# Wide experts of a mixture-of-experts layer: weights loaded two k-tiles by 1024 columns, column blocks worked in pairs, two buffers for activated gate and product

## What is computed

```python
def swiglu(h, w1, w3, w2):
    return (jax.nn.silu(h @ w1) * (h @ w3)) @ w2

def moe_swiglu(h, router_w, w1, w3, w2):
    logits = (h @ router_w).astype(jnp.float32)
    top_val, top_idx = lax.top_k(logits, TOP_K)
    gates = jax.nn.softmax(top_val, axis=-1)
    dense_gate = jnp.sum(jax.nn.one_hot(top_idx, N_EXPERTS, dtype=jnp.float32) * gates[..., None], axis=-2).astype(h.dtype)
    out = jnp.zeros_like(h)
    for e in range(N_EXPERTS):
        out = out + dense_gate[..., e:e + 1] * swiglu(h, w1[e], w3[e], w2[e])
    return out
```

## Time and profile before

| | |
|---|---|
| median of three runs | 1856.14 us |
| the profiled execution | 1855.47 us |
| its span, first to last instruction | 1853.6 us |
| mean granted TensorE clock | 0.977 |
| TensorE busy in the span | 1697.7 us (92%) |
| VectorE, ScalarE | 851.4 us (46%), 742.3 us (40%) |
| mixture-of-experts stage | about 912 to 1850 us |
| one wide and one narrow expert | 232.3 us (from 1041.1 to 1273.4 us) |

### The profile page before, as it was taken

How to read it: one execution, slowest core, us unless ns; L and a number is a source line. 1 busy time by engine, 2 the same in 40 slices (tenths; PEclk the granted TensorE clock), 3 DMA queues, 4 the chain that set the end, 5 groups by cost and what they waited for, 6 DMA issues and landing times.

```text
span 1853.6 us, 22005 instructions
## 1 busy us (share of the span) xinstructions
PE 1697.7 (92%) x9050; PEld 1201.8 (65%) x9050; DVE 851.4 (46%) x994; ACT 742.3 (40%) x918; POOL 26.1 (1%) x27
## 2 busy tenths in 40 slices
PE   6998898999999989989999977999779997799976
PEld 5877585888888868757778523885238852388622
DVE  4334726232233354263798402884028840288401
ACT  5332535222232235355677302773027730277301
POOL 0000000000000001030000000000000000000000
PEclk9999998999999999999899999999999999999999
DMA  9644133632223245162799899998999989999896
GB/s 336 202 161 135 46 114 121 210 102 91 92 99 105 91 153 171 37 180 92 269 336 376 335 409 394 377 386 333 409 395 390 369 339 409 394 374 382 336 410 267
DMA packets 238637, 473.82 MB, mean 256 GB/s; under 512 B 16121, under 2 KB 115377, under 8 KB 238529
## 3 DMA queue, kind: packets, MB, share of 16 engines
q1 hardware_dynamic: 238144, 471.38, 70.3%
q0 software_dynamic: 384, 0.95, 0.2%
HBM read 471.25 MB, written 1.05 MB: 255 GB/s over the span
## 4 chain that ended last, share of the span: by engine, by line
PE 73%; DMA 17%; DVE 5%; ACT 3%; issue 1%; SPq 1%; ACTq 0%; DVEq 0%
PE bank L608 19%; PE bank L609 19%; PE bank L610 19%; DMA raw_weights<-in_moe_w 16%; PE bank L2460 4%; PE bank L675 2%; PE bank L2477 1%; PE bank L2356 1%; PE bank L2395 1%; PE bank L465 1%; DMA raw_weights<-in_ev_w_in 1%; PE bank L888 1%; ACT split_high L587 1%; DVE split_low L1802 1%; PE bank L683 1%
## 5 line engine op out<-in xcount | busy, mean ns | idle before, releaser
L608 PE MATMUL bank<-h_high,split_high 128*128 128x512 f32 (+1 forms) x832 | 317.1, 381 | 7.4 <-DVE h_low L522 3.9
L609 PE MATMUL bank<-h_low,split_high 128*128 128x512 f32 (+1 forms) x832 | 314.4, 378 | 0.0
L610 PE MATMUL bank<-h_high,split_low 128*128 128x512 f32 (+1 forms) x832 | 314.1, 378 | 0.0
L1802 DVE TENSOR_TENSOR split_low<-raw_weights,split_high 128x2048 fp32r<-128x2048 f32 x112 | 256.3, 2289 | 79.2 <-ACT split_high L1548 78.4
L592 DVE TENSOR_TENSOR split_low<-raw_weights,split_high 128x1024 fp32r<-128x1024 f32 x118 | 144.0, 1225 | 292.3 <-ACT split_high L587 292.3
L1548 ACT ACTIVATE split_high<-raw_weights 128x2048 fp32r<-128x2048 f32 x110 | 211.0, 1918 | 77.7 <-PE bank L610 75.0
L2460 PE MATMUL bank<-raw_weights,xe_narrow 128*64 128x512 f32 (+1 forms) x1024 | 209.2, 546 | 36.0 <-DMA raw_weights<-in_moe_w 35.4
L587 ACT ACTIVATE split_high<-raw_weights 128x1024 fp32r<-128x1024 f32 x118 | 124.1, 1056 | 188.8 <-PE bank L610 183.5
L608 PEld LDWEIGHTS bank<-h_high,split_high 128*128 128x128 f32 x832 | 158.5, 191 | 40.8 <-issue 7.7
L2460 PEld LDWEIGHTS bank<-raw_weights,xe_narrow 128*64 128x64 f32 x1024 | 67.9, 136 | 168.7 <-issue 89.5
L610 PEld LDWEIGHTS bank<-h_high,split_low 128*128 128x128 f32 x832 | 158.4, 190 | 28.8
(11 more groups left out here) (303 smaller groups left out, 2225.4 us busy)
## 6 DMA issues: line engine op xcount, KB each, us to landing
raw_weights<-in_moe_w SPq DMA_DIRECT2D x336, 1024.0 KB, 8.5
raw_weights<-in_w_mod SPq DMA_DIRECT2D x48, 1024.0 KB, 6.3
raw_weights<-in_ffn_w SPq DMA_DIRECT2D x33, 1024.0 KB, 5.3
raw_weights<-in_ev_w_in SPq DMA_DIRECT2D x10, 1024.0 KB, 10.2
raw_weights<-in_od_w_in SPq DMA_DIRECT2D x8, 1024.0 KB, 6.7
raw_weights<-in_ev_w_out SPq DMA_DIRECT2D x4, 1024.0 KB, 7.1
raw_weights<-in_od_w_out SPq DMA_DIRECT2D x4, 1024.0 KB, 8.2
overlay<-in_rpb SPq DMA_DIRECT2D x32, 64.0 KB, 3.0
```

The costliest lines, as they stand in the source:

```text
L608: pe.matmul(ps, wh, xh, start=first, stop=False)
L609: pe.matmul(ps, wh, xl, start=False, stop=False)
L610: return pe.matmul(ps, wl, xh, start=False, stop=last)
L1802: dve.tensor_tensor(lo, RAW[:, u % NRAW, :], hi.bitcast(F32), ALU.subtract).then_inc(S("e_low"), 1)
```

## The change

All experts, wide and narrow, now share the order by pairs of blocks. For a wide expert:

- **Units.** A unit of `a` or `b` is two k-tiles by 1024 columns (4 KB pieces) and serves both blocks of a pair; pair 3 (block 6) keeps four k-tiles by 512 columns. The number of units, 42, the six raw buffers and the three pairs of split buffers stay.
- **Order.** a0 b0 a1 b1 d0 a2 b2 d1 a3 b3 d2 d3 by pairs, with four units in an item of pairs 0 to 2 and two in one of pair 3. A pair uses PSUM banks 0 and 2 (`a`) and 1 and 3 (`b`), the next pair the same ones again, with waits for `esilu` and `ge_free` per block.
- **Turns.** `turn(2p - 2)` stands behind the first half of the units of `a` of pair p, `turn(2p - 1)` behind the second half. For pairs 1 and 2 that is two units apart, for pair 3 one. `turn` itself has the same waits as before.
- **ScalarE and VectorE.** The silus, the high and low parts of the turned product and the products are put behind units by formulas in `u`.
- **Buffers.** `GE` and `SIL` become two each; the second ones lie in `MROW`, which is free by then. `silu` and `product` wait for one block less.
- **Seams.** The combination behind a narrow expert uses banks 1, 3, 6 and 7, as it now falls into the middle of the first `a` item. `gather` moves behind the low part of unit 4 (it was behind unit 3). `turn_onehots` comes behind unit 7 (it was behind unit 3), the `gates` behind unit 14 (it was behind unit 11).

Numbers of instructions on TensorE, ScalarE, VectorE and of DMAs don't change. The core of the diff, first the units and the buffers:

```diff
+def blocks(p):
+
+    return tuple(j for j in (2 * p, 2 * p + 1) if j < JE)
+
+def pair_units(p):
+
+    return 2 * len(blocks(p))
...
+        GE = [X[:, 4:6, 0:256], MROW[:, 0, :].rearrange("p (a n) -> p a n", a=2)]
+        SIL = [X[:, 6:8, 0:256], MROW[:, 1, :].rearrange("p (a n) -> p a n", a=2)]
...
+                    k, n, c = (2, 1024, 1024 * p) if pair_units(p) == 4 else (4, 512, 1024 * p)
```

ScalarE:

```diff
+                    for u in range(NU):
+                        if u >= 2 or b or e:
                             act.wait_ge(*raw_full(b, e, u))
                             act.wait_ge(S("e_slots"), NU * wide_before(b, e) + u + 1)
                             act.activation(esplit(u)[0], RAW[:, u % NRAW, :], ACT.Copy).then_inc(S("e_high"), 1)
+                        if u == END["b", 0] + 2 and e == 0:
                             onehot_turned()
+                        for j in range(JE):
+                            p, second = j // 2, j % 2
+                            if u == END["a", p] + 2 + 2 * second:
+                                act.wait_ge(*item_used(b, e, ("a", p)))
+                                silu(e, j, 2 * second, 256)
+                            if j < JE - 1 and u == AT["a", p + 1] + pair_units(p + 1) // 2 * (1 + second) + 2:
+                                gt_high(e, j)
```

VectorE:

```diff
+                        if u == 4 and e >= 1:
                             gather(e - 1)
+                        if u == 14 and b == 0 and e == 0:
                             gates()
+                        for j in range(JE):
+                            p, second = j // 2, j % 2
+                            if j < JE - 1 and u == AT["a", p + 1] + pair_units(p + 1) // 2 * (1 + second) + 2:
+                                gt_low(e, j)
+                            if u == END["b", p] + 2 + second:
+                                dve.wait_ge(*item_used(b, e, ("b", p)))
+                                product(e, j, 2 * second + 1, 256)
```

TensorE, first a unit of an up projection (`up`), then the order:

```diff
+                    for h, j in enumerate(blocks(p)):
+                        if q == 0 and kind == "a" and p >= 1:
+                            pe.wait_ge(S("esilu"), blocks_before(b, e) + 2 * p - 1 + h)
+                        if q == 0 and kind == "b" and p >= 1:
+                            pe.wait_ge(S("ge_free"), blocks_before(b, e) + 2 * p + h)
+                        for k in range(nk):
+                            kk = nk * q + k
+                            a = slice(UNIT // nk * k + 512 * h, UNIT // nk * k + 512 * h + 512)
+                            last = three(pe, PS[2 * h + (kind == "b")][:, :], XEH[:, plane(e), kk, :],
+                                         XEL[:, plane(e), kk, :], hi[:, a], lo[:, a], kk == 0, kk == KT - 1)
+                    last.then_inc(S("e_slots"), 1)
...
+                            up(e, kind, p, q)
+                            if kind == "a" and p == 0 and e >= 1 and q == 1:
                                 combine_last(e - 1)
+                            if kind == "a" and p >= 1 and q == half - 1:
...
+                                turn(e, 2 * p - 2)
+                            if kind == "a" and p >= 1 and q == 2 * half - 1:
+                                turn(e, 2 * p - 1)
+                        if (kind, p) == ("b", 0) and e == 0:
                             pe.wait_ge(S("onehot"), b + 1)
                             pe.wait_ge(S("grow"), 2)
                             turn_onehots()
```

## The result

The changed kernel takes 1868.44 us (median of nine runs) against 1856.14 us: a ratio of 1.0068, with an interval of 1.0058 to 1.0079 (2 us either way). The forecast was 1865.5 us, the way was right, and 2.9 us were missing.

A forecast was written before the change was run, and what follows sets the result against it. It took narrow experts as bound by DMA, wide ones by TensorE. Span 1853.6 - 0.4 + 7.5 + 1.8 + 0.6 = 1863.1 us, plus 1.9 for the execution and 0.7 for the median: 1865.6, stated as 1865.5 us, range 1855 to 1876.

The forecast's parts named there:

- The bound: In the kernel before, narrow experts are bound by the DMA and wide experts by TensorE.
- Part 1: At three handovers from narrow to wide experts, 4 KB pieces land unit 0 0.12 us earlier: -0.4 us.
- Part 2: In wide experts the order by pairs adds no new wait in pairs 1 and 2, with 0.9 us slack: 0.
- Part 3: In pair 3, turn(5) waits for gt_low(4), 1.9 us in each of four wide experts: +7.5 us.
- Part 4: Seams: first expert's one-hot transposes lose their cover, +1.8 us; gates stall more, +0.6 us; gather behind unit 4, 0.
- No stall: Rival: in pair 3 gt_low(4) comes in time, leaving only the seams, 1858 us; chance 0.19.
- faster: Rival: handovers shrink, unit 0 lands 0.7 us earlier, the clock stays, no pair 3 stall: 1848 us; chance 0.08.
- Clock lost: Rival: each new 1.9 us stall drops TensorE's clock, 11 us on top, 1877 us; chance 0.06.
- a clock under 1.0 behind the stall: Sign that the forecast is wrong: granted clock below 1.0 behind the pair 3 stall in wide experts.

The follow-up runs named there:

- the turn repaired: Changed kernel with turn(5) of pair 3 behind unit 34 instead of 33, and its product's high and low parts one unit later: 1859.94 us.
- both repairs: Changed kernel with turn(5) behind unit 34, one-hot transposes behind unit 3 again and gates in the first narrow expert: 1853.75 us, 0.9985 of before.
- the seams: Changed kernel with one-hot transposes behind unit 3 again and gates at the start of the first narrow expert, pair 3 left alone: 1864.06 us.
- the longer stall: Changed kernel with gt_low(4) on VectorE behind the low part of unit 36 instead of 35: 1891.57 us, 1.0194 of before.
- the twins with the early combination: Narrow expert's combination moved ahead of the next wide expert's unit 0: on the kernel with both repairs 1848.44 us; on the kernel before, gates in narrow expert, 1849.81 us.
- the buffers alone: Kernel before with only two buffers each for GE and SIL and the shortened waits of silu and product: 1855.84 us, 1.0002 of before.
- the twin of before with the early combination: Kernel before with gates in the first narrow expert and a narrow expert's combination ahead of the next wide expert's unit 0: 1849.81 us.

## Why the prediction was right, and what it missed

- **The bound** (narrow: DMA, wide: TensorE). Right: the narrow stretches changed by 1.0 us in all, while TensorE's waits in a wide expert came out as time, and the repairs took them away again.
- **Part 1, 4 KB pieces: -0.4 us.** Three handovers of 4.88, 4.89 and 4.88 us instead of 5.04, 5.04 and 5.03: -0.5 us. The size of the effect on the loads was put too small: ScalarE, waiting for each landing, starts a unit every 2.57 us (1156.50 - 1153.93), where I had taken 2.59 against 2.71 us from the rates. It didn't matter, as only unit 0 counts.
- **Part 2, no other wait of the order by pairs.** Right. The run with the turn repaired and the one with both repairs have no new row.
- **Part 3, the turn: +7.5 us.** 7.6 us, four times 1.9, and 8.5 us came back when it was taken away. The walk was right in its steps, each within 0.2 us.
- **Part 4.** Transposes 1.7 us (forecast 1.8), gates 0.56 us (0.6), `gather` nothing.
- **What was missed** is the term for the clock. The waits sum to 7.6 + 1.7 + 0.6 - 0.5 = 9.4 us, the forecast's 9.5; the medians moved 12.3 us. The step that failed is the rival: I let the clock decide for all stalls of 1.9 us or for none, and gave the first a chance of 0.06, from two gaps of 1.46 us. In the profiles of the changed kernel and of five of the experiments (the turn, the seams, the longer stall and the twins with the early combination), 20 gaps of PE are between 1.88 and 2.54 us long, and 9 of them are followed by a spell at 1.2 GHz; of the gaps of 4.8 to 5.1 us, all. The right term was a share of the stalls times 1.7 us; with 9 of 20 and six such gaps in the changed kernel it would be 4.6 us, an estimate, where its profile has two spells (3.4 us) and 1.0 us less at the handovers. That this holds all of the missing 2.9 us is argued, not shown for the median.
- **The rivals.** "No stall" would have given 1858, "faster" 1848; the trace excludes both, as the stalls are there and the handovers keep their 4.9 us. "Clock lost" happened behind one of the four turns in the changed kernel and behind two of four with the seams repaired, three of eight. The forecast had named a clock under 1.0 behind the stall as a sign that it is wrong; for one stall of four it came. It was also to decide by whether the stall is nearer to 5.04 or to 1.46 us, and no such rule holds for gaps of about 2 us here.

## What to carry to other kernels

When an order of work is taken over from one case to another (here from narrow experts, which wait for the loads, to wide ones, which wait for TensorE), check the odd last piece of the pattern: the chain "split behind unit u - 3, low part, then the evacuation" has room for two units between turns and none for one. Work that one engine does in another's gap has a price as soon as it moves out of it, so ask of each gap in a trace what will be standing in it afterwards. And look for idle time of the engine that bounds the next stage: moving 1.9 us of its work into it and keeping it busy brought 0.6% against the kernel before, with the repairs, where the change of the loads brought the handovers 0.5 us.

## What the runs showed of the hardware

- A gap of TensorE of about 2 us costs more than its length: behind 9 of 20 such gaps the granted clock was half for a spell, with a loss of some 1.7 us each. Behind the three gaps of 1.46 and 1.47 us (two in the kernel before, one with the buffers alone) and one of 1.80 us (the twin of before with the early combination) the clock stayed, behind all 25 of 4.8 to 5.1 us it fell. The Trainium skill, "TensorE: Matmul & The Clock Gate", section "Why this matters for your kernels", warns of idle gaps only above a length that none of these 20 reached; the runs show that shorter ones aren't safe.
- Matmuls whose result is thrown away can pay for themselves: with 8 of them in each handover (2.11 us) the clock stayed at 1.00 behind all three, where it was 1.00, 1.00 and 0.83 without them. The medians are 3.7 us apart; 1.7 us of that is seen in the profiles.
- With 4 KB pieces the units of a handover land every 2.57 us, with 2 KB pieces every 2.72 us, 6% apart. The latter is the start of this row of the kernel before, less that of ScalarE's unit in the earlier trace rows (1148.12 - 1145.40):

```profile
1148.12 1.91 ACT L1548 ACTIVATE h_high<-raw_weights 128x2048 fp32r<-128x2048 f32 x1 [0.80 <-DMA raw_weights<-in_moe_w]
```
